# A transformer kernel in two blocks: the first block's normalised groups turned during later heads, and the head of the second attention laid beside the input product

## What is computed

```
out_a = swa_sink_attention(...)          # 8 window heads  -> 512 columns
out_b = blocked_causal_attention(...)    # 4 dense heads   -> 256 columns
out_c = blocked_causal_attention(...)    # 4 latent heads  -> 256 columns
mixed = concat([rmsnorm(out_a, g_a), rmsnorm(out_b, g_b), rmsnorm(out_c, g_c)])
x = x + rmsnorm(mixed @ w_out, attn_post_norm)      # then a gated MLP with a convolution
```

```
h = modulate(rmsnorm_2(x, g_mix), sh1, sc1)
q, k, v, bg, cg, hv = split(h @ w_in)
q, k = apply_rope_2(q), apply_rope_2(k)
att  = windowed_attention(q, k, v, k_c, v_c, sink)  # blocks of 128 queries, 3 blocks of keys, 256 context keys
conv = bg * conv3(cg * hv)
x = x + gt1 * (concat([att, conv]) @ w_out)         # then 16 experts, each with its top 128 tokens
```

## Time and profile before

| | us |
|---|---|
| median of 3 runs | 2665.41 |
| lowest and highest | 2663.39, 2666.45 |
| the profiled execution | 2671.69 |
| its span in the trace | 2669.9 |
| TensorE, DVE, ACT, POOL busy | 2476.4, 1612.8, 1231.3, 678.5 |
| mean granted TensorE clock | 0.964 of full |

### The profile page before, as it was taken

The page is one execution under the profiler, slowest core; times in us unless marked ns, Lnnn a source line. Parts: engine busy times, 40 slices in busy tenths (PEclk is TensorE's granted clock), DMA queues, the critical chain, the costliest instruction groups (busy, mean ns, idle before and its releaser), DMA issues.

```text
span 2669.9 us, 32983 instructions
## 1 busy us (share of the span) xinstructions
PE 2476.4 (93%) x11388; PEld 1927.5 (72%) x11388; DVE 1612.8 (60%) x2441; ACT 1231.3 (46%) x1802; POOL 678.5 (25%) x396
## 2 busy tenths in 40 slices
PE   5999889979799999999999999979997899999996
PEld 1887467768678877877778777856674688888885
DVE  4031697655553355575542535477346899999997
ACT  4021353343443322333333421267443788888886
POOL 0211110004244467334456422220130011111100
PEclk9999899989899999899999999989998899999998
DMA  6010000022122244222222220100127899999995
GB/s 274 18 46 16 32 1 1 0 79 80 63 95 94 94 176 186 79 79 83 93 108 94 82 76 32 48 1 1 49 87 271 329 392 396 396 396 396 396 386 212
DMA packets 86490, 383.06 MB, mean 143 GB/s; under 512 B 7981, under 2 KB 9181, under 8 KB 71521
## 3 DMA queue, kind: packets, MB, share of 16 engines
q1 hardware_dynamic: 81648, 364.45, 36.2%
q0 software_dynamic: 4752, 17.43, 2.4%
HBM read 360.79 MB, written 21.05 MB: 143 GB/s over the span
## 4 chain that ended last, share of the span: by engine, by line
PE 65%; issue 15%; DVE 8%; POOL 7%; ACT 3%; DMA 1%; POOLq 0%; ACTq 0%; SPq 0%; DVEq 0%
PE ps L896 7%; PE ps L898 7%; PE ps L897 7%; PE ps L1210 6%; PE ps L1212 6%; PE ps L1211 6%; POOL w_lo L2448 5%; PE ps L866 2%; PE ps L729 2%; POOL a_lo L2452 2%; PE ps L786 2%; PE ps L788 2%; PE ps L787 2%; PE ps L721 2%; PE ps L1085 1%
## 5 line engine op out<-in xcount | busy, mean ns | idle before, releaser
L2448 POOL TENSOR_TENSOR w_lo<-arena,w_hi 128x1024 fp32r<-128x1024 f32 x188 | 457.7, 2436 | 784.1 <-ACT w_hi L1413 784.1
L2333 DVE TENSOR_TENSOR e_lo<-arena,e_hi 128x1024 fp32r<-128x1024 f32 x384 | 452.8, 1219 | 41.8 <-ACT e_hi L1711 29.4
L1711 ACT ACTIVATE e_hi<-arena 128x1024 fp32r<-128x1024 f32 x384 | 403.6, 1061 | 107.7 <-PE ps L1212 107.7
L896 PE MATMUL ps<-h_hi,w_hi 128*128 128x512 f32 x848 | 342.2, 403 | 28.6 <-DVE tiny L2017 13.1
L1413 ACT ACTIVATE w_hi<-arena 128x1024 fp32r<-128x1024 f32 x188 | 198.1, 1054 | 357.9 <-PE ps L898 357.9
L897 PE MATMUL ps<-h_lo,w_hi 128*128 128x512 f32 x848 | 336.4, 397 | 0.0
L898 PE MATMUL ps<-h_hi,w_lo 128*128 128x512 f32 x848 | 336.0, 396 | 0.0
L896 PEld LDWEIGHTS ps<-h_hi,w_hi 128*128 128x128 f32 x848 | 162.8, 192 | 73.0 <-issue 28.7
L1210 PE MATMUL ps<-e_hi,x_hi 128*128 128x512 f32 x512 | 203.5, 397 | 5.1 <-DVE x_lo L2328 4.8
L2030 DVE SCALAR_TENSOR_TENSOR arena<-ps,cols,arena 128x511 f32<-128x511 f32 x88 | 63.8, 745 | 235.3 <-ACT arena L1479 235.3
L1212 PE MATMUL ps<-e_lo,x_hi 128*128 128x512 f32 x512 | 200.5, 392 | 0.0
...
## 6 DMA issues: line engine op xcount, KB each, us to landing
arena<-in_w_up SPq DMA_DIRECT2D x108, 1024.0 KB, 8.0
...
```

The source lines that it names most:

```text
L896: pe.matmul(out, w_hi[:, q, w], hi, start=start, stop=False)
L1711: act_e.activation(e_hi[:, (2 * sl + a) % RING, :], slot[sl][:, a * D:(a + 1) * D], ACT.Copy).then_inc(s_ehi, 1)
L2333: v.tensor_tensor(e_lo[:, r, :], slot[sl][:, a * D:(a + 1) * D], e_hi[:, r, :].bitcast(F32), ALU.subtract).then_inc(s_elo, 1)
L2448: gp.tensor_tensor(w_lo[:, q, :], slot[c][:, q * D:(q + 1) * D], w_hi[:, q, :].bitcast(F32), ALU.subtract).then_inc(s_wlo, 1)
```

## The change

First block: `mixed` is normalised group by group while later heads are computed. ACT's squares of the window group come at the block ends of the window attention, its root after unit 7 of dense head 0, its scaling in head 1; the first dense group follows in heads 4 and 5. The transposes are cut in 16 pairs of a column block k and a half of the tokens (`PAIRS`), each of four transposes into bank 7. Twelve pairs are put behind units 3, 5 and 7 of heads 1, 2, 3, 6 and 7 (`TURN_AT`); pairs 12 and 13 and two late ones lie inside output parts 0 and 1, which are cut at k=6. The dense values get bank 6 alone. The dense heads are written out on TensorE, ACT and DVE, as are the window blocks on ACT.

Second block: staging of query block 0 and the scores of units 0 to 3 lie in the second half of the last input tile, ACT's exponentials and DVE's normalisations of these units before the last convolution product; query block 1 is staged inside group 0, and POOL's split of the convolution and of two weight parts follows the sink columns, one piece for each group.

```diff
-        (m_parts,) = split_views(("m_parts", 64, [2, 16384]))
-        m_hi, m_lo = m_parts[:, :, 0:KT * HALF], m_parts[:, :, KT * HALF:2 * KT * HALF]
+        m_dense0, m_dense1, m_swa0, m_swa1 = split_views(("m_dense0", 64, [2, 4, HALF]), ("m_dense1", 80, [2, 4, HALF]), ("m_swa0", 144, [2, 4, HALF]), ("m_swa1", 160, [2, 4, HALF]))
...
+        PAIRS = [(m, half) for ms in (range(4), (4, 5)) for half in range(2) for m in ms] + [(6, 0), (7, 0)]
+        TURN_AT = {8 + 5: 0, 8 + 7: 1, 16 + 3: 2, 16 + 5: 3, 16 + 7: 4, 24 + 3: 5, 24 + 5: 6, 24 + 7: 7, 48 + 3: 8, 48 + 5: 9, 48 + 7: 10, 56 + 3: 11}
+
+        def mixed_part(m, half, low):
+
+            part = (m_swa0, m_swa1)[half] if m < 4 else (m_dense0, m_dense1)[half]
+            return part[:, low, m % 4, :]
+
+        def pair_columns():
+
+            return ps[:, 7, :]
+
+        def value_bank(w, dense):
+
+            return 6 if dense else 6 + w % 2
...
+        def score_bank(u):
+
+            return (0, 4, 6, 0)[u] if u < 4 else 2 * ((u + 1) % 2)
...
-                        after(s_o, -1, w, 2)
+                        after(s_o, 0 if isdense(w) else -1, w, 1 if isdense(w) else 2)
...
                         i.then_inc(s_pv, 1)
+                    if u in hooks:
+                        hooks[u]()
...
+            def pair_turned(p):
+
+                k, half = PAIRS[p]
+                pe.wait_ge(s_gna, 4 * half + 4 if k < 4 else 4 * half + 12 if k < 6 else 16)
+                if k >= 6:
+                    pe.wait_ge(s_gn, 4)
+                pe.wait_ge(evv, T_MT + p)
+                for e in range(2):
+                    for j in range(2):
+                        i = pe.transpose(ps[:, 7, (2 * e + j) * P:(2 * e + j + 1) * P], mixed[:, 4 * half + 2 * e + j, k * P:(k + 1) * P], ident)
+                    i.then_inc(tps, 1)
+
+            def late_turned():
+
+                pe.wait_ge(s_gn, 8)
+                for c in range(2):
+                    for j in range(4):
+                        i = pe.transpose(ps[:, 4 + c, j * P:(j + 1) * P], mixed[:, 4 + j, (6 + c) * P:(7 + c) * P], ident)
+                    i.then_inc(s_flip, 1)
...
-            with pe.Fori(0, CH // 2 - 1) as m:
-                for b in range(2):
-                    units(m * 16 + (U_DENSE + 8 * (b + 1)), dense(2 * m + (b + 1), 1 - b), dense(2 * m + b, b))
-            units(U_ATT2 - 8, dense(CH - 1, 1), dense(CH - 2, 0))
+            for h in range(1, CH):
+                units(U_DENSE + 8 * h, dense(h, h % 2), dense(h - 1, 1 - h % 2),
+                      {u: (lambda u=u: pair_turned(TURN_AT[8 * h + u])) for u in range(8) if 8 * h + u in TURN_AT})
             units(U_ATT2, None, dense(CH - 1, 1))
 
-
-            pe.wait_ge(s_gn, 8)
-            pe.wait_ge(s_gna, 8)
-            for k in range(KT):
-                turn(T_MT + k, lambda h, j: mixed[:, 4 * h + j, k * P:(k + 1) * P], 4)
-            pe.wait_ge(evv, T_OUT)
-            pe.wait_ge(eva, T_OUT)
+            pe.wait_ge(s_exp, U_ATT2)
+            pe.wait_ge(evv, T_MT + 12)
+            pe.wait_ge(eva, T_MT + 12)
...
+            output_part(0, {1: lambda: pair_turned(12), 4: lambda: pair_turned(13)}, range(6))
+            output_part(1, {2: late_turned}, range(6))
+            pe.wait_ge(evv, T_OUT)
+            pe.wait_ge(eva, T_OUT)
+            for i in range(2):
+                output_part(i, {}, range(6, KT))
...
-            keep_clock(6)
-            pe.wait_ge(s_rot, 10)
-            pe.wait_ge(s_cv, 4)
-
-            pe.wait_ge(s_ks, 8)
...
-                b, nl, key = 2 * (u % 2), band_keys(n), P * max(n - 1, 0)
+                b, nl, key = score_bank(u), band_keys(n), P * max(n - 1, 0)
                 if h == 0:
                     pe.wait_ge(s_stage, NT + CH + n + 1)
-                if u >= 2:
+                if u == 0:
+                    pe.wait_ge(s_rot, 10)
+                    pe.wait_ge(s_ks, 8)
+                    pe.wait_ge(evv, T_CV + 11)
+                if u == 3:
+                    pe.wait_ge(s_max, U_ATT2 + 1)
+                if u == 4:
+                    pe.wait_ge(evv, T_CV + 12)
+                if u >= 5:
...
-            for u in range(5):
-                att_scores(u)
+            for t in range(12):
+                pe.wait_ge(evv, T_V2)
+                pe.wait_ge(eva, T_V2)
+                if t < 5:
+                    swapped2(t, q2[:, t - 1, :] if t else k2)
+                for h in range(2):
+                    tile_free(T_CV + t, h)
+                    input_part(T_CV + t, h, 12 + t, h, {2 * u: (lambda u=u: att_scores(u)) for u in range(4)} if t == 11 and h else {})
             late = None
             for b in range(2 * NT):
                 nb = len(key_blocks(b // 2))
                 for j in range(nb):
                     att_turn(b, j)
+                    if b == 0 and j == 0:
...
+            def pair_high(p):
+
+                m, half = PAIRS[p]
+                act_e.wait_ge(tps, 2 * T_MT + 2 * p + 2)
+                if p == 8:
+                    act_e.wait_ge(s_stage, NT + CH)
+                act_e.activation(mixed_part(m, half, 0), pair_columns(), ACT.Copy, scale=col("group", m)).then_inc(eva, 1)
+
+            for n in range(NT):
+                w = 2 * P if n else P
+                exps(8, 8 * n, lambda u: w, None, probs, 0)
+                if n:
+                    group_square(0, n - 1, 8 * n)
...
+            at = {2: lambda: group_square(0, NT - 1, U_DENSE), 7: lambda: group_root(0, all_rows, 8)}
+            at.update({8 + u: (lambda u=u: group_scaled(0, (2 * u - 2, 2 * u - 1))) for u in range(1, 5)})
+            at.update({17 + q: (lambda q=q: weight_high(G_OUT, 0, q, (tps, 2 * T_UQ))) for q in range(2)})
+            at.update({32 + u: (lambda u=u: [group_square(1, i, U_DENSE + 32) for i in (2 * u - 4, 2 * u - 3)]) for u in range(2, 6)})
+            at[32 + 7] = lambda: group_root(1, all_rows, 9 + 8)
+            at.update({40 + u: (lambda u=u: group_scaled(1, (2 * u - 4, 2 * u - 3))) for u in range(2, 6)})
+            at[56 + 6] = lambda: [group_square(2, i, U_ATT2 - 8 + i + 1) for i in range(4)]
+            for u, p in TURN_AT.items():
+                at[u + 1] = (lambda p=p, f=at.get(u + 1): (f() if f else None, pair_high(p)))
+            for h in range(CH):
+                exps(8, U_DENSE + 8 * h, lambda u: (u + 1) * P, lambda u: banks(2 * (u % 2), (u + 1) * P), hooks={u: at[8 * h + u] for u in range(8) if 8 * h + u in at})
...
+            group_root(2, slice(0, 4), 18 + 4)
+            for i in (4, 5):
+                group_square(2, i, U_ATT2 - 8 + i + 1)
+            for p in (12, 13):
+                pair_high(p)
+            for i in (6, 7):
+                group_square(2, i, U_ATT2 - 8 + i + 1)
+            group_root(2, slice(4, NT), 23 + 4)
+            for c in range(2):
+                act_e.wait_ge(s_flip, 3 + c)
+                act_e.activation(mixed_part(6 + c, 1, 0), ps[:, 4 + c, :], ACT.Copy, scale=col("group", 6 + c)).then_inc(s_gna, 1)
...
+                if t == 10:
+                    staged_high(0)
+                if t < 11:
+                    input_high(t + 14)
+                else:
+                    act_e.activation(apad[:, 0:1], epst, ACT.Exp)
+                    for u in range(4):
+                        att_exp(u)
...
+                    if j == 1 and b == 0:
+                        act_e.wait_ge(s_cv, 4)
+                        staged_high(1)
+                if b == 1:
+                    input_high(25)
...
+            def pair_low(p):
+
+                m, half = PAIRS[p]
+                v.wait_ge(eva, T_MT + p + 1)
+                v.scalar_tensor_tensor(mixed_part(m, half, 1), pair_columns(), col("group", m), mixed_part(m, half, 0).bitcast(F32),
+                                       ALU.mult, ALU.subtract).then_inc(evv, 1)
...
+            at = {8 + 1: lambda: group_inverse(0, slice(0, NT), 9), 40 + 1: lambda: group_inverse(1, slice(0, NT), 18)}
+            for u, p in TURN_AT.items():
+                at[u + 2 if u % 8 == 7 else u + 1] = lambda p=p: pair_low(p)
...
-            with v.Fori(1, CH) as h:
-                vc_.enter(h - 1, 8)
-                units(h * 8 + U_DENSE, dense(h), dense(h - 1))
-                vc_.leave(CH - 1)
-            units(U_ATT2, None, dense(CH - 1))
-
-            v.wait_ge(s_gq, 3)
-            v.reciprocal(grs, grs).then_inc(s_gr, 1)
-            v.wait_ge(s_gr, 1)
-            for i in range(NT):
-                for j, (c, w) in ((1, (512, 256)), (2, (768, 256))):
-                    last = v.tensor_scalar(mixed[:, i, c:c + w], mixed[:, i, c:c + w], grs[:, i, j:j + 1], None, ALU.mult)
-                last.then_inc(s_gn, 1)
-            for k in range(KT):
-                g = T_MT + k
-                v.wait_ge(eva, g + 1)
-                v.scalar_tensor_tensor(m_lo[:, :, k * HALF:(k + 1) * HALF], banks(2 * (g % 4), S).rearrange("p (a b) -> p a b", a=2), col("group", k),
```

(58 more changed lines are left out.)

203 lines of the change are left out of this document (95 added, 108 removed).

## The result

| | before | changed |
|---|---|---|
| median | 2665.93 (4 runs) | 2644.48 (4 runs) |
| lowest to highest | 2663.39 to 2670.23 | 2639.25 to 2647.44 |
| the profiled execution | 2671.69 | 2639.25 |
| mean granted clock | 0.964 | 0.973 |

The ratio is 0.9916, interval 0.9897 to 0.9935: 21.5 us faster between the medians, where 16.1 were predicted (2649). Timed once more beside the last experiments, the changed kernel gave 2644.90 beside 2666.13 (0.991, 0.989 to 0.993).

The account below looks back on a forecast made before the run. TensorE is busy nearly throughout, so time was to be had only where it waits or runs slowly, in two gaps. First block 9.9 plus second block 6.2 made 16.1 us off the median 2665.41: 2649, range 2638 to 2660.

Parts of the forecast that it names:

- the likeliest case: Whole kernel: the forecast itself, 16.1 us gained to 2649, own range 2643 to 2655, chance 0.52.
- window attention: Window attention: ACT's squares at seven block ends cost 0.2 each, 1.4 us in all.
- heads: Dense heads: moved transposes, single value bank, low parts, two roots and ACT's scalings cost 9.3 us.
- tail of the first block: After the dense heads: output product starts directly behind the value products, so part 2 starts earlier; 20.6 us gained.
- first transposes of the second attention: Start of the second attention: first transpose at 1735.5 instead of 1747.96, 12.5 us ahead.
- its groups: Second attention's groups: of the 12.5 us lead 6.3 is given back, leaving 6.2.
- the slower rival: Dense heads: written out, instructions may not be supplied fast enough; at 4 us a head 2677; chance 0.05.
- the rival of the table drain: ACT's roots between exps: table switches cost a drain of about 1.38 each, kernel at 2655; chance 0.07.
- sign of 4.5 behind the input product: Second attention: its first transpose comes some 4.5 us after the input product in the profile after.
- The collision: Second attention: POOL's subtraction delays the normalisation the next block waits on, 0.85 for each of six, 5.1 us.
- the slow clock of 2.4 put on group 1: Second attention, block 1: after TensorE idles twice for over 2 us, low clock makes it 2.4 us longer.
- The first rival: Second block keeps its lead: POOL's pieces miss the normalisations and the clock stays up; 2642, chance 0.18.

Follow-up runs that it names:

- the last experiments: The changed kernel plus POOL's subtractions in groups without staging, output part 0 finished first, its first column early, two value banks where free: 2636.14 beside 2666.13 for before.
- the other old trace: For the tail, the kernel with only the second attention changed: 2658.30; for the groups, the kernel with only the first block changed: 2654.29; both beside 2665.69.
- the early column: The changed kernel with column k=0 of output part 0 done between the last two value products: 2641.11, ratio 0.9909.

## Why the prediction was right, and where it was not

Faster, inside the range and inside the likeliest case's own range of 2643 to 2655. By its terms, in us (minus is gained):

| term | predicted | measured in the traces |
|---|---|---|
| window attention | +1.4 | -1.0 |
| heads | +9.3 | +7.0 |
| tail of the first block | -20.6 | -18.1 (-19.8 against the other old trace) |
| first transposes of the second attention | -12.5 | -12.6 |
| its groups | +6.3 | +1.9 (+0.3 against the other old trace) |
| sum | -16.1 | -22.8 (timed 21.5, by the interval 17 to 27) |

The steps were right in kind, and several sizes were not. Three terms came out better by 2.3 to 4.4 each and one worse by 2.5; that the total lies within 5 us of the forecast owes something to this offset, which was not foreseen.

- **Window attention.** From the first window exponential to the first dense one before takes 90.02, the changed kernel 89.01; every trace with the old first block lies at 90.0 to 90.1, every other one at 88.9 to 89.0. The squares cost nothing on balance, and something gained at least 1.0. ACT's loop over the blocks is written out there; that this is the cause was not tried.
- **Heads.** By the table of units: twelve pairs at 0.39 are 4.7 (5.2 predicted), and the four at unit 7 gave back 1.5 instead of 0.6. Their low parts cost 1.15 instead of 2.2. Bank and roots together are 5 x 0.24 + 2 x 0.46 = 2.1, and 2.0 was booked; ACT's scalings took 0.5 in 3-4 of head 1, as booked. So the heads' steps are right in kind, and the two that touch unit 7 are mis-sized: the prediction read that wait off one row of 0.16, where the whole distance had 0.37 to give. Heads 2 and 3 were to last 22.3 and last 22.15; head 6, also put at 22.3, lasts 21.85, since no pair stands at unit 7 of the head before it; heads without pairs last 21.3 instead of 21.0. Instruction supply, the slower rival, is excluded by the same table.
- **Tail.** The wait of 2.30 for w_lo and the 0.55 for the late pairs (0.8 predicted) came as booked. Part 2 was to start 21.35 behind the last exponential (584.3 - 562.95) and starts 23.99 behind it. Of these 2.6, the early column took back 2.36: 0.67 of wait and 1.69 of clock. The prediction counted that the slow clock of the gap would go. It did not book the single bank between the last two value products, nor that the clock would fall anew there.
- **Table loads.** ACT after head 0 in the changed kernel:

```profile
416.06 1.28 ACT L1449 ACT_TABLE_LOAD   x1
417.36 0.30 ACT L1449 ACTIVATE tiny<-tiny 128x8 f32<-128x8 f32 x1
417.68 1.28 ACT L1434 ACT_TABLE_LOAD   x1
418.97 0.37 ACT L1434 ACTIVATE arena<-ps,tiny 128x128 f32<-128x128 f32 x1
```

  Each instruction starts 0.01 to 0.02 behind the end of its load, so the rival of the table drain falls. The Trainium skill's drain of about 1.38 for each switch (ScalarE: Activation LUTs, What ACT_TABLE_LOAD costs) isn't there; the measurement decides.
- **Head of the second attention.** 12.6 for 12.5, and scores 0 waited 0.94 for 0.95. Its sign of 4.5 behind the input product was read on the old time axis; on the new one the prediction's own numbers make 1.2, and 1.04 is in the trace.
- **Groups.** The collision is as described: POOL's subtraction behind the sink column, six times, at 0.73 instead of 0.85. What failed is the slow clock of 2.4 put on group 1, and two idle times of over 2 us: the longest wait was 1.71, the clock stayed at 1.00, and group 1 lasted 8.77. Of the 4.4 between +6.3 and +1.9, 2.1 lie in group 1, 1.1 in group 0 (11.6 for 12.7) and 0.9 at POOL. The reading that DVE's normalisation ended exactly with POOL's first subtraction was 0.25 off (1765.53, and half of 4.89 behind 1762.84), which does not touch the mechanism. The first rival (the lead is kept, 2642) had its clock half right; its POOL half was wrong.

## What to carry to other kernels

A table of the distances between the same instruction of successive units, before and after, prices each edit of a software pipeline to 0.01 us and shows at which unit it strikes; where two delays strike at the same wait (bank and root here), taking one away gains nothing. When work moves ahead of a semaphore wait on GpSimd, look what VectorE does over the shared port in the next 2.4 us, staging included; a wait on the right normalisation gave back 2.2 us, and 4.3 with the work moved to groups without staging. And an idle time on TensorE can have to be priced twice, once for itself and once for the clock behind it: look for work that fits into it, as one column of the next product did here.

## What had not been expected

- A wait of 0.67, with 0.50 before it, was enough for the clock to go to 0.50 from about 574 to 577; with three matmuls in it, it stayed at 1.00. In the second attention waits of 0.94, 1.04, 0.67, 1.71 and 1.49 with work between them didn't lower it, and one of 4.33 did.
- VectorE's subtractions with two sources in SBUF stand still beside POOL's too (3.47 for 1.39), and POOL's beside theirs (2.87 for 2.35).
- In the old order the stretch of slow clock does not lie at the same instructions in each trace: group 0 took 8.08 and group 2 12.37 in the kernel before, and 10.66 and 11.31 in the kernel with only the first block changed, for the same instructions and the same waits before them (1.90 and 4.34, and 1.90 and 4.33). So a single trace is a firm baseline only for stretches at full clock. Whether the place of the slow stretch differs between kernels or between executions of one kernel, no run here shows.
